# The attention stage of a streaming encoder step, rewritten: existing key blocks, head pairs, stationary values

## The reference

```python
h = x + W_out[ rmsnorm_a(A(n1 x)) ++ rmsnorm_b(B(n1 x)) ]   # W_out: 1024 x 1024
y = rmsnorm_f(h + PEER(n2 h))
# A: 8 heads of 64, own chunk of 64 frames + the 8 chunks before, learned bias by distance
# B: 8 query heads, 2 key heads, own chunk + 2 before, ALiBi bias, one sink logit per head
# PEER: 8 retrieval heads, top 16 of 128 x 128 product keys, 16 experts per head and frame
```

## Time and profile before

| | us |
|---|---|
| Median of 3 runs | 4090.06 (4087.06 to 4090.53) |
| The profiled execution | 4093.32 |
| Its span, first to last instruction | 4091.5 |
| Attention block, to its last residual add | 999.1 |
| PE busy over the span | 2971.6 |
| DVE busy | 2380.5 |
| ACT busy | 735.7 |

### The profile page before, as it was taken

One profiled execution on the slowest core, in us unless ns is written; L12 is line 12 of the kernel. 1 busy time (PEld: TensorE's weight loads), 2 busy tenths in 40 slices (PEclk: granted clock), 3 DMA queues, 4 the chain that ended last, 5 costly groups with the idle time before them and its releaser, 6 DMA issues. The chain is left out here.

```text
span 4091.5 us, 39792 instructions
## 1 busy us (share of the span) xinstructions
PE 2971.6 (73%) x13023; PEld 1196.9 (29%) x13023; DVE 2380.5 (58%) x6206; ACT 735.7 (18%) x2363; POOL 1160.0 (28%) x1330
## 2 busy tenths in 40 slices
PE   7999999997367667667766767666766766766665
PEld 4555555565222122122112212212212211221111
DVE  2333333322767667757857866766775775775544
ACT  2333333311111111121111111111111111111111
POOL 1000000100033333333333333333333333333332
PEclk9999999965687678777768767867877876776676
DMA  4000000042199999999999999999999999999998
GB/s 182 11 11 10 16 16 16 17 151 85 78 409 407 420 407 420 411 403 412 420 401 421 405 416 404 419 418 397 417 419 398 417 421 396 421 412 415 422 421 339
DMA packets 193574, 1276.82 MB, mean 312 GB/s; under 512 B 22640, under 2 KB 26608, under 8 KB 44528
## 3 DMA queue, kind: packets, MB, share of 16 engines
q0 software_dynamic: 165888, 1208.03, 71.9%
q1 hardware_dynamic: 27504, 66.63, 4.6%
HBM read 1255.17 MB, written 12.32 MB: 310 GB/s over the span
## 5 line engine op out<-in xcount | busy, mean ns | idle before, releaser
L1132 DVE CUSTOM_DVE_ANT_0 arena<-arena,PS 128x1024 f32<-128x1024 f32 x1152 | 1383.3, 1219 | 938.1 <-DMA arena<-in_experts,arena 512.3
L1051 POOL DMA_INDIRECT arena<-in_experts,arena x1152 | 1084.3, 941 | 1975.7 <-PE PS L1286 1612.3
L1274 PE MATMUL PS<-arena 96*128 96x512 bf16 x2304 | 826.7, 459 | 848.7 <-DVE arena L1132 796.7
L1286 PE MATMUL PS<-arena 128*32 128x512 f32 x4608 | 921.5, 943 | 102.5 <-ACT arena L1117 53.7
L1274 PEld LDWEIGHTS PS<-arena 96*128 96x128 bf16 x2304 | 162.6, 104 | 1558.1 <-DVE arena L1132 1292.3
L1111 ACT ACTIVATE arena<-arena 128x4 f32<-128x4 f32 x288 | 59.5, 207 | 2075.6 <-DVE arena L1132 2048.7
L1286 PEld LDWEIGHTS PS<-arena 128*32 128x32 f32 x4608 | 163.0, 150 | 668.8 <-issue 374.4
L1308 PEld LDWEIGHTS PS<-arena 128*128 128x128 f32 x2304 | 273.1, 198 | 80.4 <-issue 78.9
L749 PE MATMUL PS<-arena 128*128 128x512 f32 (+1 forms) x720 | 288.5, 554 | 3.8 <-ACT arena L481 2.9
L1308 PE MATMUL PS<-arena 128*128 128x128 f32 x2304 | 285.8, 284 | 1.1 <-ACT arena L1068 1.1
L1117 ACT ACTIVATE arena<-arena 128x1 f32<-128x1 f32 x1152 | 244.9, 283 | 9.4
(11 more groups left out here) (168 smaller groups left out, 2091.9 us busy)
## 6 DMA issues: line engine op xcount, KB each, us to landing
arena<-in_experts,arena POOLq DMA_INDIRECT x1152
arena<-in_w_in SPq DMA_DIRECT2D x4, 2048.0 KB, 15.4
arena<-in_w_query SPq DMA_DIRECT2D x8, 1024.0 KB, 6.0
arena<-arena SPq DMA_DIRECT2D x108, 64.0 KB
h_scratch<-arena SPq DMA_DIRECT2D x9, 512.0 KB, 2.6
arena<-h_scratch SPq DMA_DIRECT2D x9, 512.0 KB, 7.9
out<-arena SPq DMA_DIRECT2D x9, 512.0 KB
arena<-in_x_prompt SPq DMA_DIRECT2D x8, 512.0 KB, 3.9
```

Of the source, the lines that this page charges most:

```text
L1051: pool.indirect_dma_start(out=uv[r], out_offset=None, in_=experts, in_offset=bass.IndirectOffsetOnAxis(ap=expert_T[t % 2][:, tok:tok + 1], ...
L1132: dve.tensor_tensor_reduce(uv[r][:, 0:D], uv[r][:, 0:D], xb(n), 1.0, 0.0, ALU.mult, ALU.add, a_dot[(n // 4) % 2][:, n % 4:n % 4 + 1]).then ...
L1274: mm = pe.matmul(PS[:, 2 + 2 * (n % 2) + c, :], pick[0:96, j:j + 1].broadcast_to([96, P]), x3[t % 2][0:96, g, 512 * c:512 * c + 512], star ...
L1286: mm = pe.matmul(PS[32 * g:32 * g + 32, ACC + c, :], wz[n % 2][:, g, 31 - f:63 - f], uv[r][:, D + 512 * c:D + 512 * c + 512], start=(f == ...
```

## The change

- **Key blocks that exist.** All keys of the prompt stay in one buffer (`k_all`), values in rings; a tile computes min(t + 1, 5) blocks for A and min(t + 1, 2) for B. The windows, their mask and POOL's shifts go.
- **Heads in pairs.** An item is a pair m of two heads whose queries and keys lie on partition halves 0 to 63 and 64 to 127; their score matmuls follow each other. There are 8 pairs per tile, 4 of A and 4 of B.
- **Softmax before the turn.** DVE reads the scores in PSUM with the bias in one instruction (`reduce`), ACT takes exponentials (`exps`), DVE divides (`normalise`), PE turns, ACT copies (`evacuate`; the fifth block of a pair goes through the first bank once that is copied, `turn_own` and `evacuate_own`).
- **Values stationary.** `weigh` holds a head's values (128 x 64) and streams the probabilities, the two heads to PSUM partitions 0 to 63 and 64 to 127. The output comes out turned; the eight transposes go.
- **Norms behind the projection.** The gain is multiplied into `w_out` once. PE projects A and B halves into four banks; the squares are summed by matmuls with a column of ones; DVE applies the inverse root in the residual add (`residual`).
- **Pieces.** One piece of the next tile's projection goes with each of the pairs 0 to 6. The norm of tile t + 2 is taken at the end of tile t; there are three x buffers.
- **Sample streams.** Scores are matmuls of 64 rows by 32 columns, eight tiles of the array; values stay per head. The two biases become one of 432 columns.
- **SP.** When the ninth tile's projection is copied, all of `w_query` and `subk` are loaded, then the bias and the caches of streams 0 and 1.
- Loops over tiles and streams are written out instead of running on the engines.

The diff, cut to its core (first constants and buffers, then SP, DVE, ACT, PE):

```diff
+V_RING, VB_RING = 6, 3
+Z_IN = 3 * AW + P
...
+BLOCKS = (0, 1, 3, 4, 2)
+PIECES = range(7)
+PIECE_AT = {m: m for m in PIECES}
...
+OUT_ORDER = ((1, 0, 2), (1, 1, 3), (0, 0, 6), (0, 1, 7))
...
+        k_all = carve(4, NT_PROMPT * P)
+        kb_all = carve(NT_PROMPT * P)
+        v_ring = [carve(AW) for _ in range(V_RING)]
+        vb_ring = [carve(P) for _ in range(VB_RING)]
+        x_sb = [carve(D) for _ in range(3)]
+        xn = carve(KD, P)
...
+                            for k in range(KD):
+                                sp.dma_start(w_query_sb[:, k, :], w_query[k * P:(k + 1) * P, :]).then_inc(w_query_ready, 16)
+                            sp.dma_start(subk_sb.rearrange("p a b -> p (a b)"), subk).then_inc(w_query_ready, 16)
+                            sp.wait_ge(s_read, 16 * NT_PROMPT)
+                            sp.dma_start(bias_s_sb, bias_s).then_inc(bias_s_in, 16)
+                            load_keys(0)
+                            sp.wait_ge(kv_stored, 16 * 14)
+                            load_values(0)
+                            load_keys(1)
+                            load_values(1)
...
+                def residual(t, i):
+                    group, half, bank = OUT_ORDER[i]
+                    cols = slice(512 * half, 512 * half + 512)
+                    dve.wait_ge(wo_psum, 4 * t + i + 1)
+                    if i >= 2:
+                        dve.wait_ge(h_ready, 4 * t + 2)
+                    dve.scalar_tensor_tensor(out=x_sb[t % 3][:, cols], in0=PS[:, bank, :], scalar=rstd[:, 1 + group:2 + group],
+                                             in1=x_sb[t % 3][:, cols], op0=ALU.mult, op1=ALU.add).then_inc(h_ready, 1)
...
+                def reduce(t, m):
+                    pair, w = 8 * t + m, width(t, m)
+                    dve.wait_ge(s_psum, pair + 1)
+                    for h in range(2):
+                        c = 2 * m + h
+                        if pair >= 2:
+                            dve.wait_ge(pT_psum, 2 * (pair - 2) + h + 1)
+                            if has_own((pair - 2) // 8, (pair - 2) % 8):
+                                dve.wait_ge(own_psum, owns(pair - 2))
+                        if m < 4:
+                            s, bias, floor = flat(2 * h)[:, 0:w], bias_a_sb[:, c, A_KEYS - w:A_KEYS], LOWEST
+                        else:
+                            s, bias = PS[:, h, 0:w], bias_b_sb[:, 4 * h + m - 4, B_KEYS - w:B_KEYS]
+                            floor = sink_sb[:, c - 8:c - 7]
+                        dve.tensor_tensor_reduce(sc[2 * (m % 2) + h][:, 0:w], s, bias, 1.0, floor, ALU.add, ALU.max,
+                                                 m_sb[:, c:c + 1]).then_inc(s_read, 1)
+                    dve.wait_ge(s_read, 2 * pair + 2)
+                    dve.tensor_scalar(nm[:, 2 * m:2 * m + 2], m_sb[:, 2 * m:2 * m + 2], -1.0, None, ALU.mult)\
+                       .then_inc(nm_ready, 1)
...
+                def normalise(t, m):
+                    w, pair = width(t, m), slice(2 * m, 2 * m + 2)
+                    dve.wait_ge(e_ready, 2 * (8 * t + m) + 2)
+                    if m >= 4:
+                        dve.wait_ge(es_ready, 4 * t + m - 3)
+                        ch.mark(dve.tensor_tensor(den[:, pair], den[:, pair], es[:, 2 * m - 8:2 * m - 6], ALU.add))
+                        ch.settle()
+                    ch.mark(dve.reciprocal(rcp[:, pair], den[:, pair]))
                     ch.settle()
+                    for h in range(2):
+                        s = sc[2 * (m % 2) + h][:, 0:w]
+                        dve.tensor_scalar(s, s, rcp[:, 2 * m + h:2 * m + h + 1], None, ALU.mult).then_inc(p_ready, 1)
...
+                for t in range(NT_PROMPT):
+                    if t:
+                        residual(t - 1, 2)
+                    reduce(t, 0)
+                    if t:
+                        residual(t - 1, 3)
+                    for m in range(8):
+                        normalise(t, m)
+                        if m < 7:
+                            reduce(t, m + 1)
+                        if m in PIECE_AT:
+                            piece(t + 1, PIECE_AT[m])
+                        if t == 0 and m == 3:
+                            dve.wait_ge(w_out_in, 16)
+                            for k in range(KD):
+                                dve.tensor_scalar(w_out_sb[:, k, :], w_out_sb[:, k, :], g_ab_sb[:, k:k + 1], None, ALU.mult)\
+                                   .then_inc(gw_ready, 1)
+                    keys(t + 1)
+                    out_rms(t)
+                    residual(t, 0)
+                    residual(t, 1)
+                    if t + 2 < NT:
+                        norm(t + 2)
+                    ch.restart()
...
+                for t in range(NT_PROMPT):
+                    exps(t, 0)
+                    for m in range(8):
+                        if m < 7:
+                            exps(t, m + 1)
+                        if m == 4:
+                            output(t, 0, OA)
+                        evacuate(t, m)
+                        if m in PIECE_AT:
+                            piece(t + 1, PIECE_AT[m])
+                        if has_own(t, m):
+                            evacuate_own(t, m)
+                    output(t, 1, OB)
+                    queries(t + 1)
+                    out_rms(t)
+                    if t + 2 < NT:
+                        norm(t + 2)
...
+                def scores(t, m):
...
+                    w = width(t, m)
+                    k0 = (t + 1) * P - w
+                    for at in range(0, w, 4 * P):
+                        n = min(w - at, 4 * P)
+                        for h in range(2):
+                            rows = slice(64 * h, 64 * h + 64)
+                            keys = k_all[rows, m, k0 + at:k0 + at + n] if m < 4 else kb_all[rows, k0:k0 + n]
+                            bank = 2 * h + at // (4 * P) if m < 4 else h
+                            mm = pe.matmul(PS[:, bank, 0:n], qT[rows, m * P:(m + 1) * P], keys, start=True, stop=True)
+                    mm.then_inc(s_psum, 1)
...
+                def weigh(t, m):
...
+                    for k in range(n):
+                        for h in range(2):
+                            if m < 4:
+                                v = v_ring[(t + 1 - n + k) % V_RING][:, (2 * m + h) * HD:(2 * m + h + 1) * HD]
+                                out = PS[64 * h:64 * h + 64, OA, m * P:(m + 1) * P]
+                            else:
+                                v = vb_ring[(t + 1 - n + k) % VB_RING][:, h * HD:(h + 1) * HD]
+                                out = PS[64 * h:64 * h + 64, OB, (m - 4) * P:(m - 3) * P]
+                            mm = pe.matmul(out, v, pT[:, h, k, :], start=(k == 0), stop=(k == n - 1))
...
+                def out_squares(t):
+                    for g in range(2):
+                        pe.wait_ge(sq_ready, 2 * t + g + 1)
+                        for k in range(4):
+                            mm = pe.matmul(PS[:, SSQ, 2 * P + g:2 * P + g + 1], xn[:, 4 * g + k, :], ones,
+                                           start=(k == 0), stop=(k == 3))
+                    mm.then_inc(ssq_psum, 1)
...
+                def stream_scores(b):
...
+                    for c0, n, rhs, chunk in ((0, CA, lambda rows, j: ckT_sb[p][rows, j, :], 0),
+                                              (CA, FR, lambda rows, j: k_all[rows, j, fr], 0),
+                                              (CA + 2 * FR, FR, lambda rows, j: kb_all[rows, fr], 4),
+                                              (CA + 3 * FR, CB, lambda rows, j: ckbT_sb[p][rows, :], 4)):
+                        for j in range(4):
+                            for r in range(2):
+                                rows, q0 = slice(64 * r, 64 * r + 64), (chunk + j) * P + b * FR
+                                mm = pe.matmul(PS[32 * j:32 * j + 32, 2 * p + r, c0:c0 + n], qT[rows, q0:q0 + 2 * FR],
+                                               rhs(rows, j), start=True, stop=True)
...
+                def stream_values(b):
...
+                    for j in range(4):
+                        at = slice(j * P + b * FR, j * P + b * FR + FR)
+                        for i in range(3):
+                            for r in range(2):
+                                head = slice((2 * j + r) * HD, (2 * j + r + 1) * HD)
+                                v = cv_sb[p][:, i, head] if i < 2 else vnew_sb[p][0:FR, head]
+                                w = pT[:, r, i, 32 * j:32 * j + FR] if i < 2 else pT[0:FR, r, 3, 32 * j:32 * j + FR]
+                                pe.matmul(PS[64 * r:64 * r + 64, OA, at], v, w, start=(i == 0), stop=(i == 2))
...
+                scores(0, 0)
+                for t in range(NT_PROMPT):
+                    for m in range(8):
+                        if m < 7:
+                            scores(t, m + 1)
+                        if m:
+                            weigh(t, m - 1)
```

(19 more changed lines are left out.)

873 lines of the change are left out of this document (358 added, 515 removed).

## The result

The changed kernel takes **3858.9 us** (median of four runs, 3857.8 to 3861.1) against 4090.3 for the kernel before in the same session (4087.1 to 4094.9): ratio 0.943, 95% interval 0.942 to 0.945.

What follows compares the result with a forecast made beforehand. PE was taken to bound the prompt tiles. Tiles to 588 us, 98.5 to stream 0, streams 119 and last projection 22.5 gave 828 against 999, 171 less: forecast 3920 us, range 3865 to 4000.

Steps and rivals of the forecast that it cites:

- last projection: Attention block's end: output copies, transposes and scaling go, one copy and the squares stay; 22.5 us, from 29.4.
- PE's work in a tile: Full prompt tile: 71 us of PE work, with a pair of heads at one head's price in scores and weighing.
- rival (2): Prompt tiles: array halves don't overlap, each A and B block costs 8 x 0.21 more, 77 us: 3997; chance 0.07.
- Waits in a tile: Full prompt tile: PE waits 5.3 us at pairs 0 and 1 and 2.7 at the tile's end.
- Clock in a tile: Prompt tile heads stay sparse, so the lower PE clock costs a full tile 5 us (0 to 10).
- rival (4): Better: clock holds at tile heads (-35), loads land with little wait (-10): 3870 us; chance 0.17.
- Streams: Eight sample streams: 119 us, from 134; first 20.7, six loops 91, last 7.4.
- The ring: Stream loop of scores 3.1, DVE 2.0, exponentials 2.5, copies 1.2, values 6 (4 to 12), gaps 0.4: 15.2 us.
- rival (1): Sample streams get longer: a small pass costs 0.14, not 0.05 to 0.08, adding 80 us: 4000; chance 0.15.
- Order on the SP queue: Tile 7: w_query and subk loads ahead of stream 0's bias and keys make PE wait 15 us (8 to 18).
- Hidden edits: Prompt tiles: norms and residual adds behind the projection cost nothing; scaling the gain into w_out costs tile 0 1 us.
- The slower rival (3): TensorE drops to its lower clock within tiles; from a third of its work the change loses, half gives 4180; chance 0.04.

Runs made afterwards that it cites:

- The run with 61 us of idle time: Changed kernel with projection pieces two pairs later and the output projection's fourth quarter ahead of the next tile's first scores: 3908.9 us, ratio 0.956.
- the one with 36 and a lower clock: Changed kernel with pieces two pairs later, fourth quarter early, both heads scoring on the same rows and weighing one after the other: 3958.0 us, ratio 0.967.

## Why the prediction was right, and where it was not

| term | forecast | measured |
|---|---|---|
| first scores read | 58 | 56.2 |
| tile 0 | 62 | 58.8 |
| tiles 1 to 3 | 69, 72, 75 | 66.6, 69.4, 72.1 |
| tiles 4 to 7 | 84 each, 83 to the wait | 77.6, 77.5, 78.9, 78.9 |
| wait for stream 0's keys | 15 | 16.0 |
| streams | 119 | 91.5 |
| last projection | 22.5 | 21.4 |
| end of the block | 828 | 764.8 |

Two steps of the prediction failed. One is a size: the streams were summed to 119 us from prices of small passes and short steps that were too dear, and took 91.5. The other is a reading: the clock was charged to the tiles as if it followed PE's idle time, 5 us a full tile and 35 in all, and at most 12 were lost. Neither takes the forecast below its range by itself; both together with shorter waits in the tiles do.

**PE's work in a tile: right.** 71 us were summed for a full tile, 72.0 measured. Each piece of it holds: a pair at one head's price in scores (1.28) and weighing (1.25 for 1.22), with the earlier trace rows the right rows to read them from, the squares at 1.7 for 2, a missing block at 2.7 us (tiles 0 to 3 rise by 2.7 to 2.8) for 3. The runs that undo the pairing show its cause; they lose 33.3 and 10.5 us, not the 77 of rival (2) (45 blocks at 8 x 0.21 are 76), since part of it lies under waits and part still overlaps.

**Waits in a tile: right place, too large.** The forecast had 5.3 us at the first pairs and 2.7 at the tile's end. The first is 4.5 (0.27, 2.83, 1.42); the second is 0.9 (0.52 here, and two of 0.19 at pairs 2 and 3). Over tiles 4 to 7 PE is idle for 19 us where 32 were forecast; one more us of work per tile takes 4 of these 13 back.

**Clock in a tile: the reading that failed.** A full tile was charged 5 us "as the sparse stretch is longer but has less work in it". The row of tile 5 has a clock of 1.00, and all prompt tiles together lost at most 12 us to it, against 55 before. The charge read the lower clock of the earlier trace rows as a matter of PE's idle time. The run with 61 us of idle time and the one with 36 and a lower clock show that this reading was wrong: it took half-array passes one by one, besides a sparse head, to get back to the 55 us. What lowered the clock in the kernel before stays open; its scores were such passes, its weighing was not. The clock half of rival (4) is what happened: it priced the whole charge at 35 us, and at most 12 were lost, so some 23 came back. (With its 10 us for the loads, rival (4) comes to 3875, not 3870; the loads did not come early.)

**Streams: the size that failed, 27.5 us, the larger miss.** The ring was drawn rightly, and PE idles in it where the forecast said; every term but the copies was too dear. Scores 1.9 for 3.1: a small pass costs 0.030 at the lower level and 0.019 at the upper one (1.89 and 1.22 us for 64), and the 0.05 was taken from four passes of 512 columns on two halves, with no row for eight tiles side by side. Values 4.3 for 6: 0.05 a pass without changes of shape, where 0.08 was taken; the charge for the changes, 0.07 to 0.3, holds with 0.12. DVE 1.6 for 2.0, exponentials 1.9 for 2.5. The range gave the values a lower end and the other steps none. With 0.030 and 0.073 per pass, rival (1), which asked for 0.14, falls.

**Order on the SP queue: right.** 15 us forecast, 16.0 measured, and 17.5 come back when the loads go behind.

**Hidden edits: right.** PE's waits in the tiles name no residual and no norm; the last projection ends 21.4 us after the streams, 22.5 forecast. Nothing behind the block changed.

**The slower rival (3)** went the other way in the tiles, for the reason above. In the streams it was right that the clock is low: 0.61, and 0.56 before. (Half of 535 is 268, so its price at half is 4188, not 4180.)

So of the 63 us by which the block ended earlier than forecast, 27.5 are the streams' small passes and short steps; 35 lie ahead of the wait for the keys: some 23 of the clock, the rest in waits, in tile 0 and in the start, less the 4 of work.

## What to carry to other kernels

Half-array passes placed beside each other gained their time here, and in a sparse stretch they went with a higher clock than the same passes one by one; so when a change fills the array better, don't carry the old stretch's clock over. Price a many-tile pass from many-tile passes or not at all, and give its range the floor of full overlap. When a stage is a ring of dependent steps, software-pipelining it by one more turn is the next gain, but ask at once which transfer the longer ring had hidden.

## What the hardware showed that was not expected

- Score passes of two row halves overlap even when four of one half are followed by four of the other (1.29 us against 1.28 alternating); of the weighing passes on column halves, four and four do (0.59 either way), ten and ten only in part (1.95 against 1.25).
- Sixty-four passes in tiles of 64 rows and 32 columns take 1.22 us at the upper clock level and 1.89 at the lower, start to start, less than a factor of two.
- A change of tile shape between value passes costs 0.11 to 0.13 us at the lower clock level (0, 4 and 8 changes: 2.55, 3.05, 3.49 us).
- The head of a tile with unpaired half-array passes, busy for 87% of its time, ran at a clock of 0.76; the same tile's head with the passes in pairs, busy for 76%, at 0.85.
